# Two-matmul pairs between the blocks of a TensorE-bound transformer kernel, fewer split sums of squares, and two reordered pieces of scalar and vector work

## The chip, the cores and the metric

One core of a Trainium2 chip runs the whole program in one launch. The metric is the device time of an execution in microseconds, the median over several executions of the same kernel. Next to the timed executions stands one execution that was recorded by the hardware profiler.

## The reference

The input is one sequence of 256 tokens, 1024 wide, in fp32. A first half has two pre-norm layers: layer 0 mixes tokens by attention (eight stick-breaking heads, eight softmax heads), layer 1 by retention, and each is followed by a gated feed-forward network (FFN) of inner width 2816. A second half has two hybrid layers with a convolution branch, a latent-attention branch (MLA) and a dilated-attention branch of three groups, merged under gates. What the change touches is this, cut to its core:

```python
def rmsnorm(x, g):                       # sums of squares over the features
    return x * rsqrt(mean(x * x, -1) + eps) * g

def retention_mixer(h, w_in, gn_gain, w_o, pos):
    q, k, v, g = split(h @ w_in)         # q, k rotated; o normalised per head by mean of squares
    return (silu(g) * o) @ w_o

def swiglu(h, w_gate_up, w_down):
    gt, up = split(h @ w_gate_up)
    return (silu(gt) * up) @ w_down

def hybrid_layer(x, ...):
    proj = rmsnorm(x, norm_g) @ w_in
    dq, dk = rmsnorm(per head of 64)     # 24 tiles of 128 rows: dqk
    ...                                  # MLA scores, dilated scores, outputs
    merged = g_a * (y_a @ w_out_a) + g_b * (y_b @ w_out_b) + g_c * (y_c @ w_out_c)
    return x + merged @ w_o
```

## The kernel before

Everything lies transposed: features on the 128 partitions, the 256 tokens along the free axis. Each weight matrix is cut into blocks of 128x1024 values, eight 128x128 tiles in a block. A block is one DMA into `raw` (four slots). ScalarE copies it into a high part `whi` (L1158, `hi`), VectorE subtracts to get the low part `wlo` (L1670, `lo`), and TensorE multiplies each tile in three matmuls, high by high, high by low and low by high (L512, L513, L514 in `run`). A block is thus 24 matmuls with 256 moving columns of the rounded fp32 type. The moving operand is `h` (normalised x), `ah` (the gated product in the FFN), `yh` or `mh` (in the merges), each with its low half beside it. `run_late` does the same for the first two tiles of some output projections (L539 to L541). All engines follow an order written out by hand and meet at semaphores. A tile result lies in one of four slots in turn, `slot_free` tells that it was read, `blk_done` that a block's matmuls are over. The tile numbered g cannot begin before the tile g-2 was read, since two share a bank pair `G`.

Between the blocks stand short matmuls in plain fp32. They sum squares over partitions with a matrix of ones (`ones`, or `bones` with ones in each head's 64 rows). Plain fp32 matmuls have two records each in the trace. The places that matter here:

- `in_halves(to, w, moving, start)` issues a 256-column fp32 matmul as two of 128 columns (all on L898). It is called by `ret_sum` (retention norm), by `d_sums` (the 24 head norms of a hybrid layer, one after each block) and by `mla_scores`.
- `entry_sums` (L966, L967) sums squares at the entry of each hybrid layer, in halves.
- `ffn(b, g, n)` on TensorE runs `run_two`, two further blocks and then a hardware loop over 10 groups of four blocks; FFN1 has its first four blocks by themselves and then loops from the third group on. The `down` projection follows each FFN at once, without other work between.
- The merge of a hybrid layer is 4 x 3 turns of three blocks. Ahead of the second block of the first turn stands `pair_outs(7)`, the last attention output (L1102). In the first turn, ahead of the third block, TensorE waits on `y_lo` for the last low half of `yh`.
- The entry of the retention layer: blocks 0 to 3 run on x before it is normalised (`run_unnormed`), so their results are multiplied by 1/rms on VectorE (`by_root`, L1930) and get a shift added on ScalarE (L1372, a loop of four that waits for `q_scaled`). Only after that loop does ScalarE read out block 4 (L1401).
- The entry of FFN1 is alike. There VectorE has the products of group 0 (`up_gate` L2006, `up_low` L2012), then `ffn(..., first=1)`: for each half of a group `lo`, the product of gate and up (L1901), `lo`, the product's low half (L1905), and in some turns a reduction for the modulation vectors (L1678, by the table `FFN1_DOTS`).

## Time and profile before

| | us |
|---|---|
| timed executions | 1467.92, 1468.67, 1471.16 |
| median | 1468.67 |
| profiled execution, its own time | 1464.42 |
| its span, first to last instruction | 1462.6 |
| TensorE busy in the span | 1441.0 (99%) |
| VectorE busy | 1043.7 (71%) |
| ScalarE busy | 848.6 (58%) |
| mean granted TensorE clock | 0.997 |

The profiled execution's own time is 1.8 us more than its span. Its own time is also 4.25 us below the median of the timed ones and 3.5 us below the lowest. A matmul's duration in the trace is modelled and overlaps the next one's, so the pace of TensorE is to be read from starts, or from how many instructions a stretch holds, and not from busy time.

### The profile page before, as it was taken

Reading aid. Unit: us, or ns where it says so; the run is one execution under the profiler, and the core shown is the slowest. Engines: PE = TensorE matmul, PEld = TensorE weight load, DVE = VectorE, ACT = ScalarE, POOL = GpSimd, SP = SyncE. Lnnn points to the kernel's source line nnn. Section 1 sums busy time; section 2 is a strip of 40 time slices with the busy share of each in tenths; the row PEclk is TensorE's granted clock in tenths of the full one; section 3 lists DMA queues with packets and bytes.
Section 4 is the critical chain, followed back from the end, with each engine's and each line's share of the span. In section 5 each row is a group of like instructions: output and inputs, shape, how many; then the busy total and the mean of one; then the engine's idle time right before and its main releaser. Section 6 shows DMA issues by size and latency. Waiting matters only on the chain.

```text
span 1462.6 us, 30445 instructions
## 1 busy us (share of the span) xinstructions
PE 1441.0 (99%) x11704; PEld 1371.9 (94%) x11704; DVE 1043.7 (71%) x1861; ACT 848.6 (58%) x1482; POOL 92.0 (6%) x136
## 2 busy tenths in 40 slices
PE   8999999999999999999999999999999999999999
PEld 6887999999989999999998989899999898989999
DVE  2888898987776678765666757876576684787664
ACT  4465666555456756545566766554456675656543
POOL 0101011110000000000020000410000000031000
PEclk9999999999999999999999999999999999999999
DMA  9867699997665377666563554345666355434663
GB/s 364 325 208 224 218 337 336 340 348 229 200 233 156 116 216 228 190 191 196 188 232 117 162 169 145 97 123 185 190 189 209 115 172 165 143 96 130 188 200 118
DMA packets 81186, 292.06 MB, mean 200 GB/s; under 512 B 9185, under 2 KB 10465, under 8 KB 80946
## 3 DMA queue, kind: packets, MB, share of 16 engines
q1 hardware_dynamic: 68274, 244.31, 51.6%
q0 software_dynamic: 11792, 42.77, 8.8%
q10 hardware_dynamic: 1008, 3.41, 0.7%
q8 instruction: 80, 1.31, 0.4%
q14 instruction: 32, 0.26, 0.1%
HBM read 289.40 MB, written 1.05 MB: 199 GB/s over the span
## 4 chain that ended last, share of the span: by engine, by line
PE 89%; DVE 7%; ACT 2%; issue 2%; DMA 0%; SPq 0%; DVEq 0%; ACTq 0%
PE G L512 22%; PE G L513 22%; PE G L514 22%; PE G L571 3%; PE G L572 3%; PE G L573 3%; DVE wlo L1670 2%; PE Tp L898 2%; PE O L1102 1%; PE G L593 1%; ACT whi L1158 1%; PE Tp L952 1%; PE S L1004 1%; DVE aw L1678 1%; PE Tp L686 1%
## 5 line engine op out<-in xcount | busy, mean ns | idle before, releaser
L1670 DVE TENSOR_TENSOR wlo<-raw,whi 128x1024 fp32r<-128x1024 f32 x444 | 546.0, 1232 | 257.2 <-ACT whi L1158 255.4
L1158 ACT ACTIVATE whi<-raw 128x1024 fp32r<-128x1024 f32 x444 | 468.8, 1058 | 216.7 <-PE G L514 160.7
L512 PE MATMUL G<-h,whi 128*128 128x256 f32 x2064 | 583.5, 283 | 4.8 <-DVE at L2319 1.6
L513 PE MATMUL G<-h,whi 128*128 128x256 f32 x2064 | 572.8, 278 | 0.0
L514 PE MATMUL G<-h,wlo 128*128 128x256 f32 x2064 | 572.8, 278 | 0.0
L512 PEld LDWEIGHTS G<-h,whi 128*128 128x128 f32 x2064 | 389.4, 189 | 10.6 <-issue 2.2
L513 PEld LDWEIGHTS G<-h,whi 128*128 128x128 f32 x2064 | 388.0, 188 | 0.7 <-issue 0.5
L514 PEld LDWEIGHTS G<-h,wlo 128*128 128x128 f32 x2064 | 387.8, 188 | 0.0
L1678 DVE CUSTOM_DVE_ANT_0 aw<-aw,cs,cols 128x1024 f32<-128x1024 f32 x80 | 101.4, 1278 | 0.0
L512 PE MATMUL G<-ah,whi 128*128 128x256 f32 x352 | 97.2, 276 | 0.0
L513 PE MATMUL G<-ah,whi 128*128 128x256 f32 x352 | 97.2, 276 | 0.0
L514 PE MATMUL G<-ah,wlo 128*128 128x256 f32 x352 | 97.2, 276 | 0.0
L488 POOL TENSOR_TENSOR bias<-dist,slopes 128x256 f32<-128x256 f32 (+1 forms) x48 | 47.3, 1002 | 538.3 <-DVE mn L2272 528.8
L512 PE MATMUL G<-yh,whi 128*128 128x256 f32 x288 | 80.2, 278 | 0.0
L513 PE MATMUL G<-yh,whi 128*128 128x256 f32 x288 | 80.0, 278 | 0.0
L514 PE MATMUL G<-yh,wlo 128*128 128x256 f32 x288 | 80.0, 278 | 0.0
L571 PE MATMUL G<-whi,h 128*128 128x512 f32 x192 | 76.8, 400 | 1.4 <-ACT mqk L1267 1.4
L471 POOL DMA_DIRECT2D aw<-in_ada x80 | 42.4, 530 | 536.3 <-DVE mod L1678 502.0
L572 PE MATMUL G<-whi,h 128*128 128x512 f32 x192 | 75.6, 394 | 0.0
L573 PE MATMUL G<-wlo,h 128*128 128x512 f32 x192 | 75.6, 394 | 0.0
L512 PEld LDWEIGHTS G<-ah,whi 128*128 128x128 f32 x352 | 66.1, 188 | 0.0
L513 PEld LDWEIGHTS G<-ah,whi 128*128 128x128 f32 x352 | 66.1, 188 | 0.0
(408 smaller groups left out, 2334.1 us busy)
## 6 DMA issues: line engine op xcount, KB each, us to landing
raw<-in_w SPq DMA_DIRECT2D x444, 512.0 KB, 3.8
aw<-in_ada POOLq DMA_DIRECT2D x80, 512.0 KB, 5.4
adaw<-in_ada SPq DMA_DIRECT2D x8, 1024.0 KB, 15.5
sn<-in_uq ACTq DMA_DIRECT2D x2, 768.0 KB, 4.3
x<-in_x SPq DMA_DIRECT2D x1, 1024.0 KB, 5.3
pt<-in_ukv ACTq DMA_DIRECT2D x2, 512.0 KB, 5.4
out<-x SPq DMA_DIRECT2D x4, 256.0 KB, 2.3
dec<-in_dec ACTq DMA_DIRECT2D x1, 512.0 KB, 7.3
```

The lines of the kernel that those rows point to most:

```text
L471: pool.dma_start(aw[:, r % ADA_SLOTS, :], a["ada"][16 + r]).then_inc(ada_raw[r % ADA_SLOTS], 16)
L488: pool.tensor_tensor(bias[:, DIST[grp]], dist[:, DIST[grp]], slopes[:, c:c + 1].broadcast_to([P, w]), ALU.mult).then_inc(bias_ready, 1)
L512: pe.matmul(o, wh, mv[:, 0:T], start=(k == 0), stop=False)
L513: pe.matmul(o, wh, mv[:, T:2 * T], start=False, stop=False)
L514: ins = pe.matmul(o, wl, mv[:, 0:T], start=False, stop=(k == k_of - 1))
L571: pe.matmul(o, hh, wh, start=(k == 0), stop=False)
L572: pe.matmul(o, hl, wh, start=False, stop=False)
L573: ins = pe.matmul(o, hh, wl, start=False, stop=(k == KT - 1))
L898: ins = pe.matmul(to[:, o:o + P], w, moving[:, o:o + P], start=start, stop=True)
L1158: act.activation(whi[:, s, :], raw[:, s, :], ACT.Copy).then_inc(w_hi, 1)
L1670: dve.tensor_tensor(wlo[:, s, :], raw[:, s, :], whi[:, s, :], ALU.subtract).then_inc(w_lo, 1)
L1678: return dve.tensor_tensor_reduce(out=w, in0=w, in1=cs[:, :], scale=1.0, scalar=cols[:, C_ADAB + n:C_ADAB + n + 1], op0=ALU.mult, op1=ALU.add,
```

## The change

Five edits. (1) A new helper `settle` issues two 128-column fp32 matmuls of `ones` by `ones` into the bank `O`, whose content nobody reads. It is called four times: in `ffn` ahead of the loop (FFN0), ahead of FFN1's loop, and in each hybrid layer's merge ahead of the third block of the first turn. (2) Sums of squares stay in halves only where nothing but the sum stands between two blocks: `ret_sum` for head 3, `d_sums` for the tiles 3 and 5 to 17 (it is called with j-1). Elsewhere (three in retention, ten in each hybrid layer) they are one 256-column matmul. `entry_sums` has its first operand whole and its second in halves. (3) `mla_scores` issues the 256-column part first and whole, then the 128-column part. (4) ScalarE's four shifts at the retention entry move behind the read-out of blocks 5 and 6, two at each. (5) At FFN1's entry VectorE does the first gate product of group 1 right after the first low half of group 0, and the reductions start two halves later.

```diff
-FFN1_DOTS = {_f: [70 + _f] for _f in range(2, 10)}
+FFN1_DOTS = {_f: [68 + _f] for _f in range(4, 12)}
...
+            def settle():
+                for _ in range(2):
+                    pe.matmul(O[:, 0:P], ones[:, :], ones[:, :], start=True, stop=True)
...
                 run(b + 2, g + 2, 2, 8, of_h)
+                settle()
                 with pe.Fori(1, FT // 2) as i:
...
-                in_halves(Tp[:, slot, 0:T], ones[:, :], sq[:, 4, :], True).then_inc(t_done, 1)
+                if hh == 3:
+                    in_halves(Tp[:, slot, 0:T], ones[:, :], sq[:, 4, :], True).then_inc(t_done, 1)
+                else:
+                    pe.matmul(Tp[:, slot, 0:T], ones[:, :], sq[:, 4, :], start=True, stop=True).then_inc(t_done, 1)
...
             run(B_FFN1 + 4, G_FFN1 + 4, 4, 8, of_h, each_k=lambda k: pe.wait_ge(h_ready, 24 + k + 1))
+            settle()
             with pe.Fori(2, FT // 2) as i:
...
+                    pe.matmul(S[:, 2, 0:T], ones[:, :], sq[:, 0, :], start=True, stop=False)
                     for o in (0, P):
-                        pe.matmul(S[:, 2, o:o + P], ones[:, :], sq[:, 0, o:o + P], start=True, stop=False)
-                        ins = pe.matmul(S[:, 2, o:o + P], ones[:, :], sq[:, KT - 1, o:o + P], start=False, stop=True)
+                        ins = pe.matmul(S[:, 2, o:o + P], ones[:, :], sq[:, KT - 1, o:o + P], start=False, stop=(o == P))
...
-                        d_sums(j - 1)
+                        d_sums(j - 1, alone=j == 4 or 5 < j < 19)
...
-                    pe.matmul(S[:, slot, 0:P], q[:, 0:P], kk[:, 0:P], start=True, stop=True)
-                    in_halves(S[:, slot, P:384], q[:, P:T], kk, True).then_inc(s_done, 1)
+                    pe.matmul(S[:, slot, P:384], q[:, P:T], kk, start=True, stop=True)
+                    pe.matmul(S[:, slot, 0:P], q[:, 0:P], kk[:, 0:P], start=True, stop=True).then_inc(s_done, 1)
...
                             pe.wait_ge(y_lo, l * 12 + 12)
+                            settle()
...
-            for b in range(4):
+            def shift(b):
+
                 act.wait_ge(q_scaled, b + 1)
                 act.activation(rqk[:, b, :], rqk[:, b, :], ACT.Identity, bias=scol[:, b:b + 1]).then_inc(q_shifted, 1)
...
                 hi(B_RET + b + 4)
+                if b in (5, 6):
+                    shift(2 * b - 10)
+                    shift(2 * b - 9)
...
             up_low(0)
+            dve.wait_ge(ah_ready, FT + 1)
+            gate_product(B_FFN1, G_FFN1, 1, 0)
             up_low(1)
+            lo(B_FFN1 + 8)
+            lo(B_FFN1 + 9)
+            product_low(1, 0)
+            lo(B_FFN1 + 10)
             dve.wait_ge(ah_ready, FT + 2)
-            ffn(B_FFN1, G_FFN1, FFN1_DOTS, 1)
+            gate_product(B_FFN1, G_FFN1, 1, 1)
+            lo(B_FFN1 + 11)
+            product_low(1, 1)
+            ffn(B_FFN1, G_FFN1, FFN1_DOTS, 2)
```

On TensorE, in the first turn of hybrid layer 0's merge, at the border of the second block (moving operand `h`) and the third (`yh`), there stood:

```order
L514 MATMUL G<-h,wlo 128x256
L512 MATMUL G<-h,whi 128x256
L513 MATMUL G<-h,whi 128x256
L514 MATMUL G<-h,wlo 128x256
L512 MATMUL G<-yh,whi 128x256
L513 MATMUL G<-yh,whi 128x256
L514 MATMUL G<-yh,wlo 128x256
```

and there stands now, with the pair at the border:

```order
L514 MATMUL G<-h,wlo 128x256
L512 MATMUL G<-h,whi 128x256
L513 MATMUL G<-h,whi 128x256
L514 MATMUL G<-h,wlo 128x256
L857 MATMUL O<-ones 128x128 x2
L512 MATMUL G<-yh,whi 128x256
L513 MATMUL G<-yh,whi 128x256
L514 MATMUL G<-yh,wlo 128x256
```

The pair came between two blocks; nothing else moved there.

On ScalarE, at the retention entry (L1329 and L1344 are the read-out of a raw block, L1158 and L1173 `hi`, L1372 and L1388 the shifts, L1401 and L1417 the read-out of blocks 4, 5, 6, ...), before:

```order
L1329 ACTIVATE rqk<-G 128x256
L1158 ACTIVATE whi<-raw 128x1024 x2
L1372 ACTIVATE rqk<-rqk,hb 128x256 x4
L1401 ACTIVATE rqk<-G 128x256
L1158 ACTIVATE whi<-raw 128x1024
L1401 ACTIVATE rqk<-G 128x256
L1158 ACTIVATE whi<-raw 128x1024
L1401 ACTIVATE rqk<-G 128x256
```

and now:

```order
L1344 ACTIVATE rqk<-G 128x256
L1173 ACTIVATE whi<-raw 128x1024 x2
L1417 ACTIVATE rqk<-G 128x256
L1173 ACTIVATE whi<-raw 128x1024
L1417 ACTIVATE rqk<-G 128x256
L1173 ACTIVATE whi<-raw 128x1024
L1388 ACTIVATE rqk<-rqk,hb 128x256 x2
L1417 ACTIVATE rqk<-G 128x256
L1173 ACTIVATE whi<-raw 128x1024
L1388 ACTIVATE rqk<-rqk,hb 128x256 x2
L1417 ACTIVATE rqk<-G 128x256
```

The read-outs of blocks 4 and 5 passed all four shifts.

On VectorE, at FFN1's entry (L2006 and L2033 `up_gate`, L2012 and L2039 `up_low`, L1901 and L1918 the gate product, L1905 and L1924 its low half, L1670 and L1689 `lo`, `ISA` the reduction), before:

```order
L2006 SCALAR_TENSOR_TENSOR af<-af,hb,sg 128x256
L1670 TENSOR_TENSOR wlo<-raw,whi 128x1024
L2012 TENSOR_TENSOR ah<-af,ah 128x256 x2
L1670 TENSOR_TENSOR wlo<-raw,whi 128x1024
L1901 TENSOR_TENSOR af<-G,sg 128x256
L1670 TENSOR_TENSOR wlo<-raw,whi 128x1024
L1905 TENSOR_TENSOR ah<-af,ah 128x256
L1678 ISA aw,mod<-aw,cs,cols 128x1024
L1678 ISA mod 128x1
L1670 TENSOR_TENSOR wlo<-raw,whi 128x1024
```

and now:

```order
L2033 SCALAR_TENSOR_TENSOR af<-af,hb,sg 128x256
L1689 TENSOR_TENSOR wlo<-raw,whi 128x1024
L2039 TENSOR_TENSOR ah<-af,ah 128x256
L1918 TENSOR_TENSOR af<-G,sg 128x256
L2039 TENSOR_TENSOR ah<-af,ah 128x256
L1689 TENSOR_TENSOR wlo<-raw,whi 128x1024 x2
L1924 TENSOR_TENSOR ah<-af,ah 128x256
L1689 TENSOR_TENSOR wlo<-raw,whi 128x1024
L1918 TENSOR_TENSOR af<-G,sg 128x256
L1689 TENSOR_TENSOR wlo<-raw,whi 128x1024
L1924 TENSOR_TENSOR ah<-af,ah 128x256
L1689 TENSOR_TENSOR wlo<-raw,whi 128x1024
```

The first product passed an `up_low` and a `lo`, and two reductions left this stretch for later.

## Rows read from the trace of the kernel before

**Rows 1.** The page: its span, and its chain that ended last by engine

```profile
span 1462.6 us, 30445 instructions
...
PE 89%; DVE 7%; ACT 2%; issue 2%; DMA 0%; SPq 0%; DVEq 0%; ACTq 0%
```

**Rows 2.** Windows: length; busy (x count) PE, PEld, DVE, ACT, POOL; clock; DMA; GB/s

```profile
172.70:346.70 174.00, 174.00 (x1538) 174.00 (x1537) 154.35 (x219) 101.64 (x134) 23.22 (x44) 1.00 0.93 331
365.80:385.80 20.00, 20.00 (x171) 20.00 (x171) 14.86 (x13) 10.02 (x16) 0.00 (x0) 1.00 0.50 154
566.40:726.40 160.00, 160.00 (x1414) 160.00 (x1413) 106.70 (x140) 82.56 (x119) 1.58 (x3) 1.00 0.67 208
976.00:1072.00 96.00, 96.00 (x818) 96.00 (x817) 57.54 (x78) 47.05 (x65) 0.00 (x0) 1.00 0.58 182
...
1344.00:1440.00 96.00, 96.00 (x849) 96.00 (x848) 61.32 (x84) 49.37 (x67) 0.00 (x0) 1.00 0.64 189
1442.40:1459.00 16.60, 16.60 (x142) 16.60 (x142) 7.18 (x10) 3.49 (x4) 0.00 (x0) 1.00 0.16 61
```

**Rows 3.** Timeline of TensorE around two single sums in halves, hybrid layer 0

```profile
765.73 0.29 PE L513 MATMUL G<-h,whi 128*128 128x256 f32 x1
...
768.32 0.28 PE L514 MATMUL G<-h,wlo 128*128 128x256 f32 x1
768.45 0.61 PE L898 MATMUL Tp<-sq,bones 128*128 128x128 f32 x4
...
769.36 0.28 PE L513 MATMUL G<-h,whi 128*128 128x256 f32 x1
...
771.52 0.28 PE L514 MATMUL G<-h,wlo 128*128 128x256 f32 x1
...
786.58 0.28 PE L514 MATMUL G<-h,wlo 128*128 128x256 f32 x1
...
787.26 0.28 PE L513 MATMUL G<-h,whi 128*128 128x256 f32 x1
```

**Rows 4.** Timeline of TensorE: a 256-column fp32 matmul before a block

```profile
761.14 0.60 PE L985 MATMUL Tp<-csq,ones 128*128 128x256 f32 x2
...
761.69 0.28 PE L513 MATMUL G<-h,whi 128*128 128x256 f32 x1
```

**Rows 5.** Timeline at the retention entry, TensorE and then ScalarE

```profile
364.61 0.28 PE L514 MATMUL G<-h,wlo 128*128 128x256 f32 x1
365.58 0.38 PE L512 MATMUL G<-h,whi 128*128 128x256 f32 x1 [0.69 <-ACT rqk L1401]
365.80 0.28 PE L513 MATMUL G<-h,whi 128*128 128x256 f32 x1
...
359.79 2.01 ACT L1158 ACTIVATE whi<-raw 128x1024 fp32r<-128x1024 f32 x2
...
363.95 1.31 ACT L1372 ACTIVATE rqk<-rqk,hb 128x256 f32<-128x256 f32 x3 [0.96 <-DVE rqk L1930]
365.17 0.36 ACT L1401 ACTIVATE rqk<-G 128x256 f32<-128x256 f32 x1
```

**Rows 6.** Timeline at FFN1's entry, TensorE and then VectorE

```profile
564.63 0.28 PE L514 MATMUL G<-h,wlo 128*128 128x256 f32 x1
565.97 0.39 PE L512 MATMUL G<-h,whi 128*128 128x256 f32 x1 [1.06 <-DVE af L1901]
566.19 0.28 PE L513 MATMUL G<-h,whi 128*128 128x256 f32 x1
...
563.57 0.75 DVE L2012 TENSOR_TENSOR ah<-af,ah 128x256 fp32r<-128x256 f32 x2
564.35 1.23 DVE L1670 TENSOR_TENSOR wlo<-raw,whi 128x1024 fp32r<-128x1024 f32 x1
565.50 0.42 DVE L1901 TENSOR_TENSOR af<-G,sg 128x256 f32<-128x256 f32 x1
```

**Rows 7.** Timeline of VectorE: the last low half of `yh`, layer 0

```profile
974.91 0.43 DVE L2294 TENSOR_TENSOR yh<-hpair,yh 128x256 fp32r<-128x256 f32 x1 [0.15 <-ACT yh L1604]
```

More of the change, by code:

```diff
@@ L970, in entry_sums @@
                         pe.wait_ge(sqf_ready, 8)
+                        pe.matmul(S[:, 1, 0:T], ones[:, :], sqf[:, 0, :], start=True, stop=False)
                         for o in (0, P):
[L972 to L973 removed]
+                            ins = pe.matmul(S[:, 1, o:o + P], ones[:, :], sqf[:, KT - 1, o:o + P], start=False,
+                                            stop=(o == P))
                     ins.then_inc(ss_done, 1)
@@ L1020, in mla_transposes, with d_sums @@
                     ins.then_inc(t_done, 1)
-                def d_sums(j):
+                def d_sums(j, alone=False):
                     slot = use_t()
                     pe.wait_ge(d_sq, l * 24 + j + 1)
-                    in_halves(Tp[:, slot, 0:T], bones[:, :], sq[:, j % 8, :], True).then_inc(t_done, 1)
+                    if alone:
+                        in_halves(Tp[:, slot, 0:T], bones[:, :], sq[:, j % 8, :], True).then_inc(t_done, 1)
+                    else:
+                        pe.matmul(Tp[:, slot, 0:T], bones[:, :], sq[:, j % 8, :], start=True, stop=True).then_inc(t_done, 1)
                 pe.wait_ge(in_hyb, 64)
@@ L1892, in _, with gate_product, product_low @@
             x_update(B_ATT_O, 8, G_ATT_O, one_each, 2, 4, later={0: [21], 1: [22], 2: [23]})
+            def gate_product(b, g, i, q):
+                gg = g + 2 * q
+                dve.wait_ge(blk_done, b + 2 * q + 2 + 4 * i)
+                dve.wait_ge(slot_free[gg % 4], taken(gg) + i)
+                dve.tensor_tensor(af[:, q, :], gslot(gg + 1), sg[:, q, :],
+                                  ALU.mult).then_inc(slot_free[(gg + 1) % 4], 1)
+            def product_low(i, q):
+                dve.wait_ge(ah_hi, ah_base[0] + i * 2 + q + 1)
+                dve.tensor_tensor(ah[:, i * 2 + q, T:2 * T], af[:, q, :], ah[:, i * 2 + q, 0:T],
+                                  ALU.subtract).then_inc(ah_ready, 1)
             def ffn(b, g, later, first=0):
```

12 lines of the change are left out of this document (2 added, 10 removed).

## The prediction

> **What bounds the kernel now.** I read the page first: its chain is TensorE for 89% and VectorE for 7% [rows 1]. So a saved matmul interval is saved time, and work on the other engines counts only where TensorE is seen to wait for it. Next I read TensorE's stream in windows, since its durations are modelled, and divided each window's length by its count of matmuls. A count includes those under way at the window's start, so I add one duration, 0.28 us, to the length [rows 2, 5]. FFN0 with its down projection: 174.28/1538 = 113.3 ns from start to start. FFN1: 160.28/1414 = 113.4. The merge of hybrid layer 1: 96.28/849 = 113.4. The merge of layer 0, the same code on the same shapes: 96.28/818 = 117.7 [rows 2]. Twenty microseconds at the retention entry (20.28/171 = 118.6, its uneven first intervals included) and the last 16.6 us of the program (16.88/142 = 118.9, its edges included) are of the slow kind too. The granted clock is 1.00 in all of them, its 2.4 GHz level, and TensorE is busy for the whole window, so neither the clock nor a wait explains it: the same stream has two paces, 4.35 ns a matmul apart, and it keeps the one that it has for hundreds of matmuls.
>
> What sets the pace? At two single sums in halves: before the first one 22 intervals take 768.32 - 765.73 = 2.59 us, 117.7 ns each, and after it 19 take 771.52 - 769.36 = 2.16, 113.7 by rounded starts [rows 3]. One pair of 128-column fp32 matmuls alone between blocks took the stream from slow to fast. There are 28 such places in the two hybrid layers. A stall works differently: after the one at the retention entry the pace is slow [rows 2, 5], after the one at FFN1's entry fast [rows 2, 6]. I read the pace after a stall as chance, which is an inference from those two.
>
> **The settling pairs (+1.8, -3.7 us).** What one costs: from the last matmul before the sum to the second after it 787.26 - 786.58 = 0.68 us, where two intervals without it would be 0.23, so 0.45 [rows 3]. Four of them are 1.8 us on the path. Nothing waits for bank `O` there, and `settle` adds no wait. In layer 0's merge the pair stands behind the wait on `y_lo`; that half was ready at 974.91 + 0.43 = 975.34, and the block in front of the pair begins at 973.9 and lasts 2.8 us, so this wait stays covered [rows 7]. What they bring: in layer 0's merge 34 blocks of 24 matmuls follow, 816 x 4.35 ns = 3.55 us, and some 48 matmuls of the output projection, 0.2 us, if the slow pace lasted until there: 3.7 us. ScalarE and VectorE can feed the fast pace, since they do so in layer 1 [rows 2]; were they late, the loss would be up to those 3.7. In layer 1's merge, FFN0 and FFN1 the profiled execution is fast already, so there the pair only costs. At the end of a merge the pace changes once more: in layer 1 the last 142 matmuls are slow behind a fast merge [rows 2]. If layer 0's output projection now does the same, 142 x 4.35 = 0.6 us come back; I count half, +0.3, bounds 0 and 0.6.
>
> [...]
>
> **The shifts (-1.7 us).** TensorE's block 6 begins late: from its predecessor's start to its own second matmul it is 365.80 - 364.61 = 1.19 us instead of 0.23, a stall of 0.96. It waited for ScalarE's read-out of block 4, which began at 365.17, behind the shifts, which wait for VectorE's `by_root` [rows 5]. Block 5 began 24 intervals (2.72) ahead of 364.73, at 362.0, so block 4 was over by about 362.1, and ScalarE was free of its two `hi` at 359.79 + 2.01 = 361.80. Without the shifts it reads block 4 out at 362.2 to 362.6, two microseconds before block 6 wants the slot. The next to be late could be `lo` of block 8, wanted at 364.7 + 2 x 2.72 = 370.2. Its `hi` (1.0 us) now ends near 363.6, its `lo` (1.2 us) follows VectorE's `by_root`, at about 366. Blocks 5 and 6 carry two shifts each afterwards, 2 x 0.4 us in a block of 2.7, beside one `hi` and one read-out: 2.2 us, which fits. So all 0.96 goes. With the stall goes what it left behind, since I saw the pace before it to be fast: some 171 slow matmuls x 4.35 = 0.74. Bounds 0.96 (the slow pace comes otherwise) and 1.7; I take 1.7, as nothing else interrupts the stream there.
>
> **The gate product (-1.35 us).** TensorE's block 7 stalls alike: 566.19 - 564.63 = 1.56 instead of 0.23, so 1.33, for the product at L1901. VectorE was busy up to it: the two low halves (563.57, 0.75 us), then `lo` (564.35, 1.23 us), then the product at 565.50 [rows 6]. Now the product stands behind the first low half, at about 563.95, and ends near 564.35, before block 7 wants the slot at 564.74. That is a margin of 0.4 us. Should the extra wait for the own low half cost 0.1, it still holds; should the product come 0.5 us late, 0.1 of the stall stays. Behind it `lo` of block 8 ends near 566.0 (wanted 567.5), of block 9 near 567.1 (wanted 570.2), the second product follows block 7 and `lo` of block 10, near 568.9, for a slot wanted at 570.2. Two reductions (1.28 each) moved out of this stretch make that room and are taken up later in a loop that has it. I take 1.33, bounds 1.2 and 1.35.
>
> **Whole sums and the score order (-0.5 us).** One 256-column fp32 matmul before a block: 761.69 - 761.14 = 0.55 us to the block's second matmul [rows 4]. The pair takes from its own start, one interval (0.12) behind 786.58, 787.26 - 786.70 = 0.56 [rows 3]. So each of 23 sums saves 0.01 to 0.02 us, as do 16 score pairs and 3 groups at the entries: 42 x 0.015 = 0.6, from 0.4 to 0.8. What pace the next block has is the larger unknown. Behind these places stand some 40 blocks of 24 matmuls, 0.10 us each between the two paces, part slow today and part fast: from -2 to +2 us if all went one way. The single pairs were kept where they work, and a pair with other work behind it shows nothing that it loses, so I take 0 for this and -0.5 for the edit.
>
> **The sum.** +1.8 - 3.7 + 0.3 - 1.7 - 1.35 - 0.5 = -5.15. The profiled execution's own time would go from 1464.42 to 1459.3.
>
> The timed executions lie 3.5 to 6.7 us above the profiled one, and the pace explains that without any other cause: in the profile FFN0, FFN1 and layer 1's merge were all fast. Slow, they would cost 1538 x 4.35 = 6.7 us, 1414 x 4.35 = 6.2 and 849 x 4.35 = 3.7 [rows 2]. The median is 4.25 above, about one merge; the highest is 6.7 above, one FFN. If that is so, the pairs pin all four stretches, and the timed executions of the changed kernel come down to its profiled one, with some 0.7 us for the short stretches that stay free: **1460.0 us**. If the 4.25 is a fixed difference of a recorded execution, the time is 1468.67 - 5.15 = 1463.5.
>
> **The rivals.** *Fixed difference*: 1463.5, as just worked out. For it speaks that all three timed executions lie above the recorded one; against it that two stretches of like code differ by just that amount. *The pair does not hold the pace*: it sets the next block fast, and the stream falls back, or the pace is set by something later. Then the 3.7 stay and the pairs cost 1.8: 1468.67 + 1.8 + 0.3 - 1.7 - 1.35 - 0.5 = 1467.2, about no change. [...] Against it speaks that fast stretches last 170 us [rows 2]; for it that none of the 28 pairs has more than one block behind it before the next short matmul. *Slower*: the state that a pair leaves depends on what it is issued from, and behind a branch into a hardware loop it is the slow one. FFN0 and FFN1, now fast, would lose 6.7 + 6.2 = 12.9 us, fixed in each execution: 1463.5 + 12.9 = 1476.4. It decides from about 8 us, so it takes both FFNs, or one with layer 0's merge unmended. No pair in the trace stands at such a branch.
>
> **How the numbers follow.** A measurement of this kernel can tell about 0.2%, 2.9 us. Pinned paces, 1457 to 1462: 55%. Fixed difference, 1462 to 1465.5: 28%. The pair does not hold: 12%, of which most within 2.9 us of before. Slower: 4%; 1% is for what I don't see. The range 1457 to 1465.5 holds the first two, 83%. Faster by over 0.2%: the first two and a little of the third, 86%; the same 10%; slower 4%.
>
> **What would show it.** In the changed profile the windows of layer 0's merge, layer 1's merge, FFN0 and FFN1 must all give 113.4 ns a matmul. The stalls before blocks 6 and 7 of the two entries must be gone, with 113 ns through the retention entry. The pair must cost 0.45. The timed executions must lie closer to the profiled one and to each other than 3.5 and 3.2 us. I am wrong if a stretch behind a pair runs at 117.7, if VectorE's new order shows a wait for `lo` of block 8 or 9, or if the 40 short blocks turned slow.

## The result and the profile after

The changed kernel takes 1478.38 us, median of 8 runs (1473.26 to 1481.88); the kernel before, beside it on the same chip, 1466.84 us (1463.35 to 1471.91, 8 runs). The ratio is 1.0079, 95% interval 1.0051 to 1.0106: slower, where 1460.0 and a range of 1457 to 1465.5 were predicted. The profiled execution took 1481.88 us. The ratios, here and below, compare whole sets of executions; where a set is skewed they differ from the quotient of the two medians, by up to 0.003. One execution of e12_ones_at_64 below took 2048.87 us at a granted clock of 0.65 and is left out of that run's numbers. The page of after, its span and its chain that ended last (compare [rows 1]):

```profile
span 1480.1 us, 30308 instructions
...
PE 87%; DVE 8%; ACT 3%; issue 2%; DMA 1%; SPq 0%; DVEq 0%; ACTq 0%
```

TensorE still bounds. Windows of after (length; busy time and count of PE, PEld, DVE, ACT, POOL; clock, DMA share, GB/s): FFN0 with its down projection, the retention entry, FFN1, the two merges, the last 16.6 us (compare [rows 2]):

```profile
180.00:350.00 170.00, 170.00 (x1445) 170.00 (x1445) 145.75 (x208) 94.62 (x125) 22.47 (x43) 1.00 0.93 323
368.00:388.00 20.00, 20.00 (x179) 20.00 (x178) 14.82 (x17) 12.04 (x20) 0.00 (x0) 1.00 0.67 209
577.00:735.00 158.00, 158.00 (x1344) 158.00 (x1343) 100.61 (x131) 77.57 (x112) 1.58 (x3) 1.00 0.64 200
992.00:1088.00 96.00, 96.00 (x817) 96.00 (x817) 58.63 (x81) 46.44 (x63) 0.00 (x0) 1.00 0.61 187
1360.00:1456.00 96.00, 96.00 (x817) 96.00 (x816) 58.65 (x81) 46.68 (x64) 0.00 (x0) 1.00 0.60 186
1459.90:1476.50 16.60, 16.60 (x143) 16.60 (x143) 7.18 (x10) 3.45 (x4) 0.00 (x0) 1.00 0.16 60
```

With 0.28 us added to each length, as in the prediction: 170.28/1445 = 117.8 ns a matmul in FFN0, 158.28/1344 = 117.8 in FFN1, 96.28/817 = 117.8 in both merges. All four stretches behind a settling pair are slow. The retention entry, which has no pair, is fast: 20.28/179 = 113.3. The granted clock is 1.00 in all of them, and TensorE has no idle time in any, so once more neither clock nor wait tells the paces apart.

The timeline of TensorE around FFN0's pair in after: two rows some distance ahead, the rows at the pair, two rows behind:

```profile
172.99 0.28 PE L512 MATMUL G<-h,whi 128*128 128x256 f32 x1
...
175.48 0.28 PE L513 MATMUL G<-h,whi 128*128 128x256 f32 x1
...
178.31 0.28 PE L514 MATMUL G<-h,wlo 128*128 128x256 f32 x1
178.43 0.60 PE L857 MATMUL O<-ones 128*128 128x128 f32 x4
178.79 0.36 PE L512 MATMUL G<-h,whi 128*128 128x256 f32 x1
178.99 0.28 PE L513 MATMUL G<-h,whi 128*128 128x256 f32 x1
...
181.11 0.28 PE L513 MATMUL G<-h,whi 128*128 128x256 f32 x1
...
183.70 0.28 PE L514 MATMUL G<-h,wlo 128*128 128x256 f32 x1
```

Between the first two rows lie 22 intervals: 2.49/22 = 113.2 ns. Between the last two lie 22 as well: 2.59/22 = 117.7. The pair itself costs what was predicted, 178.99 - 178.31 = 0.68 us where 0.23 stood. What it leaves is the opposite: it took a fast stream and made it slow. The other three do the same (FFN1's at 575.17, the merges' at 989.96 and 1357.46: fast in front, slow behind), and the pace then stays for 1390, 863 and 863 matmuls.

I counted every start-to-start interval between two 256-column matmuls of the stream: 116 to 122 ns is slow, up to 114 ns fast. Before has 2339 slow intervals, which is 10.4 us above the fast pace; after has 6276, which is 28.0 us. The difference is 17.5 us, and so is that of the spans, 1480.1 - 1462.6. The four stretches behind the pairs alone are 1486 + 1390 + 863 + 863 = 4602 slow intervals, 20.5 us. In before the one of layer 0's merge was slow already, so 3739 of them, 16.7 us, are new.

The two stalls that the other edits were made for are gone. ScalarE in after at the retention entry, and VectorE and TensorE at FFN1's (compare [rows 5, 6]):

```profile
369.52 0.38 ACT L1417 ACTIVATE rqk<-G 128x256 f32<-128x256 f32 x1 [0.40 <-PE G L514]
372.24 0.38 ACT L1417 ACTIVATE rqk<-G 128x256 f32<-128x256 f32 x1 [1.38 <-PE G L514]
...
373.47 0.90 ACT L1388 ACTIVATE rqk<-rqk,hb 128x256 f32<-128x256 f32 x2
```

```profile
571.73 0.42 DVE L1918 TENSOR_TENSOR af<-G,sg 128x256 f32<-128x256 f32 x1
572.07 0.41 DVE L2039 TENSOR_TENSOR ah<-af,ah 128x256 fp32r<-128x256 f32 x1
```

```profile
572.34 0.28 PE L514 MATMUL G<-h,wlo 128*128 128x256 f32 x1
572.45 0.28 PE L512 MATMUL G<-h,whi 128*128 128x256 f32 x1
572.56 0.28 PE L513 MATMUL G<-h,whi 128*128 128x256 f32 x1
```

ScalarE now waits for TensorE at each read-out and not the other way round, with the shifts in the gap behind. The product ends at 572.15, 0.3 us before TensorE's block 7 begins at 572.45, and its matmuls follow at 0.11.

### The profile page after: what moved, and what is told of

It is laid out like the page before. It is cut to its first block, busy times and chain, and to the rows that moved or that the text cites. A ratio compares the mean times of both kernels' runs of the same rounds, so it can differ in the third digit from the quotient of the medians.

```text
span 1480.1 us, 30308 instructions
## 1 busy us (share of the span) xinstructions
PE 1459.9 (99%) x11636; PEld 1387.2 (94%) x11636; DVE 1043.9 (71%) x1861; ACT 847.6 (57%) x1482; POOL 92.6 (6%) x136
## 4 chain that ended last, share of the span: by engine, by line
PE 87%; DVE 8%; ACT 3%; issue 2%; DMA 1%; SPq 0%; DVEq 0%; ACTq 0%
PE G L512 22%; PE G L514 21%; PE G L513 21%; DVE wlo L1689 2%; PE G L571 2%; PE G L573 2%; PE G L572 2%; ACT whi L1173 1%; PE O L1116 1%; PE Tp L904 1%; PE G L593 1%; PE Tp L962 1%; DVE aw L1697 1%; PE S L1015 1%; PE Tp L686 1%
## 5 line engine op out<-in xcount | busy, mean ns | idle before, releaser
L1689 DVE TENSOR_TENSOR wlo<-raw,whi 128x1024 fp32r<-128x1024 f32 x444 | 545.9, 1232 | 265.9 <-ACT whi L1173 264.2
L1173 ACT ACTIVATE whi<-raw 128x1024 fp32r<-128x1024 f32 x444 | 468.3, 1057 | 229.5 <-PE G L514 172.8
L513 PE MATMUL G<-ah,whi 128*128 128x256 f32 x352 | 98.9, 281 | 0.0
L512 PE MATMUL G<-ah,whi 128*128 128x256 f32 x352 | 98.9, 281 | 0.0
L513 PEld LDWEIGHTS G<-ah,whi 128*128 128x128 f32 x352 | 67.6, 192 | 0.0
L514 PEld LDWEIGHTS G<-ah,wlo 128*128 128x128 f32 x352 | 66.1, 188 | 0.0
```

The lines of the kernel that those rows point to most:

```text
L512: pe.matmul(o, wh, mv[:, 0:T], start=(k == 0), stop=False)
L513: pe.matmul(o, wh, mv[:, T:2 * T], start=False, stop=False)
L514: ins = pe.matmul(o, wl, mv[:, 0:T], start=False, stop=(k == k_of - 1))
L1173: act.activation(whi[:, s, :], raw[:, s, :], ACT.Copy).then_inc(w_hi, 1)
L1689: dve.tensor_tensor(wlo[:, s, :], raw[:, s, :], whi[:, s, :], ALU.subtract).then_inc(w_lo, 1)
```

## The experiments

A pair of the head norms (stationary matrix `bones`) had been seen to leave a fast stream; the settling pair (stationary matrix `ones`) left a slow one. In what do they differ? The head norms' pair is two halves of one sum with operand `sq`, it stands behind waits, it signals a semaphore, it writes bank `Tp`, and its stationary matrix is another tensor. In what follows F is the fast pace (113.3 ns), S the slow one (117.8), and F to S means that the stream was fast in front of an insertion and slow behind it, read in the block on either side. All medians have the kernel before measured beside them, on the same chip.

**e1_no_pairs, e2_pairs_alone, e3_pairs_as_sums, s1_kinds.** The first takes all `settle()` calls out of the changed kernel; the second puts only the four pairs into the kernel before; the third writes the pair like a head norm's sum; the fourth puts 68 pairs of seven kinds between the blocks of both merges of the kernel before.

```diff
 # e1 (the changed kernel; at all four places)
-                        settle()
 # e2 (the kernel before), s1: settle() at the four places, pair(kind) at 68
+                            settle()
 # e3 (the changed kernel)
-                for _ in range(2):
-                    pe.matmul(O[:, 0:P], ones[:, :], ones[:, :], ...)
+                pe.wait_ge(in_ones, 16)
+                for o in (0, P):
+                    ins = pe.matmul(O[:, o:o + P], ones[:, :], sq[:, 0, o:o + P], ...)
+                ins.then_inc(settled, 1)
```

> The changed kernel without its four settling pairs. Theory A (the pair of ones by ones leaves the slow pace behind it, and the four long stretches pay for it): the two stalls stay gone, nothing forces the four stretches, each has either pace by chance; the time is about 0.8 to 1.2% below the changed kernel's, 1460 to 1467 us, and the profile has 117.8 ns in at most two or three of the four. Rival B (the slow pace comes from the other edits, the whole sums, the score order or the missing stalls): the four stretches stay at 117.8 and the time stays near 1477.

> The kernel before with the four pairs and nothing else. Theory A: all four stretches run at 117.8 ns behind the pair, and with 1.8 us for the pairs and the stalls kept the time is 1478 to 1484 us, above the changed kernel's. Rival B: the pace is as before, 1467 to 1470.

> The changed kernel with each pair written as the head norms' pair is: squares as moving operand, two halves of the bank, a wait that is met already ahead of it, an increment behind it. Theory A1 (what the pair consists of decides): 113.4 ns in all four stretches and 1457 to 1463 us. Rival A2 (the place decides, such as the 24-matmul blocks around it and what the next waits are, not the pair's form): 117.8 ns in all four as in the changed kernel, 1476 to 1480.

> A screening on the kernel before: in both merges a pair between every two blocks from the third on, 68 in all, of seven kinds in two orders: plain as in the change; two halves of the bank; a met wait ahead; an increment behind; squares as moving operand; halves, wait and increment; all four. The next block's pace is read from each. If one property decides, its kinds give 113 ns and the others 118 whatever the pace was before; if the place decides, kinds do not differ. The time is about 68 x 0.45 = 31 us above before and more with slow blocks.

Without the pairs: 1464.45 us (1458.57 to 1475.62, 12 runs) beside 1467.23, ratio 0.9993 [0.9965, 1.0022]. So the pairs are the loss. In e1's profile all four stretches are fast. The pairs alone: 1475.3 us (1473.16 to 1487.05), ratio 1.0087 [1.0058, 1.0116], the whole loss of the change. Its profile shows what the changed kernel's could not: the pair does not make the stream slow, it turns the pace. FFN0 went F to S, FFN1 S to F, the first merge S to F, the second F to S. Windows of e2 in these four stretches:

```profile
180.00:347.00 167.00, 167.00 (x1420) 167.00 (x1419) 142.75 (x204) 93.32 (x123) 22.27 (x42) 1.00 0.92 323
577.00:735.00 158.00, 157.65 (x1391) 157.45 (x1390) 103.85 (x137) 80.84 (x117) 1.06 (x2) 1.00 0.66 206
986.00:1082.00 96.00, 96.00 (x850) 96.00 (x849) 60.35 (x83) 48.63 (x66) 0.00 (x0) 1.00 0.63 192
1350.00:1446.00 96.00, 96.00 (x818) 96.00 (x817) 57.90 (x79) 46.18 (x64) 0.00 (x0) 1.00 0.61 186
```

167.28/1420 = 117.8 and 96.28/818 = 117.7 behind the two that were fast; 96.28/850 = 113.3 in the first merge. Written as a sum, the pair turns the pace as well: e3 took 1476.95 us (1475.99 to 1481.57), 1.0086 [1.0059, 1.0114], with F to S, S to F, F to S, F to S. In s1, one execution of 1497.31 us, 68 of 68 insertions turned it, whatever the kind (plain, halves, met wait, increment, `sq` operand, and their sums), with 677 ns from the last matmul in front to the second behind for F to S and 685 for S to F. The form of the sum is out. All of these stand in an unbroken stream. One pair with `ones` in every kernel stands behind a stall, the last sum of retention, with 0.96 to 1.28 us over the insertion, and there all four outcomes occur: F to F in after and e1, F to S in e4 and e6, S to F in before and e2, S to S in e3 and e9.

**s2_kinds, e4_two_waits, e5_two_pairs, e6_orders_alone.** s2 is a second set of 68 insertions: one to four matmuls, two met waits ahead, the head norms' bank, `bones` as stationary matrix. e4 and e5 are the changed kernel with two met waits ahead of each pair, and with four matmuls at each place. e6 is the kernel before with the moved shifts and the moved product alone.

```diff
 # s2 (the kernel before), in both merges at each border of blocks
+                            pair(next(kinds))
 # e4
+                pe.wait_ge(in_ones, 16)
+                pe.wait_ge(in_c, 32)
                 for _ in range(2):
 # e5
-                for _ in range(2):
+                for _ in range(4):
 # e6 (the kernel before), ScalarE; VectorE's half is that of the change
+                if b in (5, 6):
+                    shift(2 * b - 10)
+                    shift(2 * b - 9)
```

> So far a pair of 128-column fp32 matmuls has always turned the pace round (72 of 72 outside the head norms), whatever its operands, bank, single wait or increment, while the head norms' pairs give the fast pace from either. Screening on the kernel before, 34 insertions in each merge in random order: 2 matmuls; 2 behind two met waits; 1, 3, 4 matmuls; one of 256 columns, without and with two waits; 2 with the head norms' matrix; 2 in the head norms' bank. Theory W (the two waits ahead of a head norm's pair make the difference): only the kinds with two waits give the fast pace from either state, the matrix and the bank turn round. Rival M (the matrix or the bank does): those kinds give fast from either. For the number: if each 128-column matmul shifts a phase, 1 and 3 keep or turn as 2 does not, and 4 keeps the pace.

> The changed kernel with two met waits ahead of each pair. Theory W: the two FFN stretches run at 113.4 ns in each execution (the merges have a third wait there already and may differ), and the time is 1456 to 1464 us. Rival M: the pair turns the pace as before, 1475 to 1480 us.

> The changed kernel with two pairs in a row at each of the four places. If a pair turns the pace round, two keep it: the stretches run at what they had ahead of the pairs, mostly fast, and the time is 1462 to 1470 us with 3.6 us for the pairs. Rival (fp32 work of any length leaves the slow pace): 117.8 ns in all four, 1478 to 1482.

> The kernel before with the moved shifts and the moved gate product alone. Theory: both stalls of 0.96 and 1.33 us are gone in the profile, and the stretches behind them have the pace that the stream had ahead of them; the median is 2 to 4 us under before, with a spread of some 10 us between executions that can hide it. Rival: the stalls come back elsewhere, the time is as before.

What s2 showed (one execution, 1499.55 us), by kind. The entries give the pace behind the insertion, first where the stream in front was fast, then where it was slow:

```
                                     from F         from S
one 128-column matmul, ones          F 4 of 4       F 1, S 1
three, ones                          F 4 of 4       F 1, S 1
two, ones, two met waits ahead       S 8 of 8       F 5 of 5
two, ones, in the head norms' bank   S 6 of 6       F 2 of 2
two, ones                            S 5 of 5       F 3 of 3
two, bones                           F 2 of 2       F 6 of 6
four, ones                           -              F 6 of 6
one 256-column, ones                 S 8 of 8       F 4, S 1
```

Two 128-column matmuls with `ones` turned the pace every time, four did so from a slow stream, one or three left a fast stream fast and had both answers from a slow one. A 256-column fp32 matmul turned the pace in 12 of 13 cases. Waits and bank count for nothing, but with `bones` a pair leaves the stream fast. e4 took 1474.81 us, 1.005 [1.0024, 1.0075]: the theory of the waits falls. e5 took 1475.53 us, 1.0036 [1.0007, 1.0064], with F to S three times and S to F once: four matmuls turn the pace as two do, and that two pairs would keep it was a miss. e6 took 1466.8 us, 1.0001 [0.997, 1.0031], its runs spread over 20 us (1457.99 to 1478.52): its retention entry is fast and free of the stall, and its FFN1 happened to be slow for 1438 matmuls, 6.4 us, more than the edits bring. With the pace left free, small edits can't be measured in this kernel.

**s3_matrices, e7_single.** s3 varies the stationary matrix alone in 68 insertions; e7 is the changed kernel with one matmul at each place instead of two.

```diff
 # s3 (the kernel before), w: ones, bones, ident or dist[:, c:c + P]
+                for k in range(n):
+                    pe.matmul(O[:, 0:P], w, ones[:, :], start=True, stop=True)
 # e7
-                for _ in range(2):
+                for _ in range(1):
                     pe.matmul(O[:, 0:P], ones[:, :], ones[:, :], start=True, stop=True)
```

> The screening so far: two met waits change nothing (13 of 13 turned the pace round), the bank neither (8 of 8), but with the head norms' matrix as stationary operand the pair gave the fast pace 8 times of 8, twice from the fast one. Here the stationary operand varies, 68 insertions on the kernel before: ones, head norms' matrix, identity, and 128-column pieces of the distance table that begin 0, 16, 32, 64 and 3584 bytes into it; also a single matmul with either of the first two. Theory P (place in the memory: ones, identity and the piece at 64 bytes begin on a multiple of 128 bytes, the head norms' matrix and the pieces at 0 and 3584 half way between two): the latter three give fast from either pace, the former three turn it round. Rival C (content, mostly zeros): the head norms' matrix and the identity give fast, all pieces of the table turn it round.

> The changed kernel with one 128-column matmul of ones by ones in place of each pair. In the screening one matmul kept the fast pace (4 of 4) and gave the fast one in one of two cases from the slow pace. So the two FFN stretches and the merge stretches, fast ahead of it, stay at 113.4 ns where the pair turned them: 1457 to 1466 us. Rival: at these places one matmul does what two do, 1475 to 1480 us.

In s3 (one execution, 1493.7 us) a pair with the identity turned a fast stream in 5 of 5 cases, like `ones`, and so did a piece of the distance table (6 of 6); other pieces of the same table, 32 to 64 bytes earlier, left it fast (9 of 9), as `bones` did (3 of 3). So it isn't what the matrix holds, it is where it lies. `ones`, the identity and the piece that turns start 128 bytes into a stretch of 256 in their partition's memory, as do the weight tiles `whi` and `wlo`; `bones` starts at 64. A single matmul with `ones` left a fast stream fast (4 of 4) and, here, a slow one slow (2 of 2); a single one with `bones` made it slow (5 of 5), the reverse of what the two do as pairs.

e7 took 1459.44 us (1458.31 to 1461.66, 12 runs) beside 1467.46 (1460.98 to 1472.75), **ratio 0.9954 [0.994, 0.9969]: faster than both kernels**, by 0.5% against before, with a spread of 3.4 us where before has 11.8. The timeline of e7 at FFN1's single matmul:

```profile
567.66 0.28 PE L514 MATMUL G<-h,wlo 128*128 128x256 f32 x1
567.77 0.38 PE L857 MATMUL O<-ones 128*128 128x128 f32 x2
567.91 0.37 PE L512 MATMUL G<-h,whi 128*128 128x256 f32 x1
568.11 0.28 PE L513 MATMUL G<-h,whi 128*128 128x256 f32 x1
```

and windows of e7: FFN0, the retention entry, FFN1, the merges:

```profile
180.00:347.00 167.00, 167.00 (x1476) 167.00 (x1475) 147.74 (x211) 97.52 (x129) 22.79 (x43) 1.00 0.94 335
361.00:384.00 23.00, 23.00 (x205) 23.00 (x204) 17.76 (x21) 14.22 (x23) 0.00 (x0) 1.00 0.59 184
569.00:725.00 156.00, 156.00 (x1379) 156.00 (x1378) 103.83 (x137) 80.69 (x117) 1.59 (x3) 1.00 0.66 208
977.00:1073.00 96.00, 96.00 (x849) 96.00 (x848) 60.47 (x84) 48.34 (x66) 0.00 (x0) 1.00 0.63 194
1341.00:1437.00 96.00, 96.00 (x849) 96.00 (x849) 60.34 (x83) 48.27 (x65) 0.00 (x0) 1.00 0.63 193
```

The single costs 568.11 - 567.66 = 0.45 us where 0.23 stood, and 167.28/1476, 23.28/205, 156.28/1379 and 96.28/849 are 113.3, 113.6, 113.3 and 113.4 ns: all these stretches are fast. Three of the singles went F to F, and FFN0's, in front of which the stream was slow, S to F. With those of s2 and s3 that makes 2 of 5 slow streams that a single with `ones` mended, so why all twelve executions lie so close together is not shown. This is the state that the prediction had forecast for the pair, at the time that it had forecast.

**e8_ones_moved, e9_singles_alone, e10_bones_aligned.** e8 moves the ones matrix 64 bytes further in the changed kernel (and all tensors behind it by 128); e9 is the kernel before with the four single matmuls only; e10 is the kernel before with `bones` moved from 64 to 128 bytes into 256 (and all tensors behind it by 128).

```diff
 # e9 (the kernel before, settle() at the four places)
+                for _ in range(1):
+                    pe.matmul(O[:, 0:P], ones[:, :], ones[:, :], start=True, stop=True)
 # e8
+        sb("pad_a", [P, 16])
         ones = sb("ones", [P, P])
+        sb("pad_b", [P, 16])
 # e10
+        sb("pad_c", [P, 16], stack=second)
         bones = sb("bones", [P, P], stack=second)
+        sb("pad_d", [P, 16], stack=second)
```

> The changed kernel with the matrix of ones 64 bytes further in the memory, nothing else. Theory P (a pair whose stationary matrix does not begin on a multiple of 128 bytes leaves the fast pace): 113.4 ns behind all four settling pairs, and 1457 to 1462 us with a spread of some 4 us. Rival (the pair's place in the program counts too, or the content): the four stretches stay slow, 1475 to 1480 us.

> The kernel before with one 128-column matmul of ones by ones at each of the four places. Both FFN stretches and the merges keep the fast pace where they come in fast. Against e7_single it still has the two stalls (0.96 and 1.33 us, and a pace by chance behind each until the single) and the split sums (0.5 us): 1461 to 1464 us. Rival: the other edits are worth nothing, 1459 to 1460.

> The kernel before with the head norms' matrix on a multiple of 128 bytes (64 further). Theory P: its single pairs between blocks now turn the pace round, so the blocks of the head norms alternate between 113.4 and 117.8 ns where they were all fast, some 14 slow blocks more, 1.5 us. Rival C (content): they all stay fast.

e8 took 1484.68 us (1481.66 to 1485.68), 1.0114 [1.0084, 1.0145]: a miss. Its pairs went F to S three times and S to F once, and the head norms' 28 pairs, whose `bones` had moved to 192 as well, left the stream slow in 28 of 28 cases, in each of which it had come in slow. A pair at 192 bytes does not leave the stream fast, so the rule on record for e8 (every place but the multiples of 128 bytes leaves it fast) is wrong. e10 met its expectation: in the kernel before these 28 pairs leave the stream fast, every one; with `bones` at 128 they turn it, every one, 16 times F to S and 12 times S to F. Two of them in a row, timeline of TensorE in e10:

```profile
792.16 0.28 PE L516 MATMUL G<-h,wlo 128*128 128x256 f32 x1
792.27 0.60 PE L900 MATMUL Tp<-sq,bones 128*128 128x128 f32 x4
792.63 0.36 PE L514 MATMUL G<-h,whi 128*128 128x256 f32 x1
792.83 0.28 PE L515 MATMUL G<-h,whi 128*128 128x256 f32 x1
...
795.42 0.28 PE L516 MATMUL G<-h,wlo 128*128 128x256 f32 x1
795.54 0.61 PE L900 MATMUL Tp<-sq,bones 128*128 128x128 f32 x4
795.91 0.37 PE L514 MATMUL G<-h,whi 128*128 128x256 f32 x1
796.11 0.28 PE L515 MATMUL G<-h,whi 128*128 128x256 f32 x1
...
798.62 0.28 PE L516 MATMUL G<-h,wlo 128*128 128x256 f32 x1
```

From a block's second matmul to its last lie 22 intervals: (795.42 - 792.83)/22 = 117.7, then (798.62 - 796.11)/22 = 114.1 with the uneven first ones. The profiled execution of e10 has a span of 1473.6, its one time is 1475.45 us. e9 took 1464.65 us, 0.9987 [0.9969, 1.0005], with a spread of 5.5 us: F to F at all four singles, and still the stall and the slow pace at the retention entry.

**s4_places, e11_mask_pair, e12_ones_at_64.** s4 takes ten places within one matrix, the distance table. e11 gives the pair of the changed kernel another stationary matrix, the causal mask, at 32 bytes into 256, and moves nothing. e12 moves the ones matrix to 64, and keeps all tensors behind it at their places into 256.

```diff
 # s4 (the kernel before): w = dist[:, c:c + P], ten values of c
 # e12
+        sb("pad_a", [P, 48])
         ones = sb("ones", [P, P])
+        sb("pad_b", [P, 16])
 # e11
-                    pe.matmul(O[:, 0:P], ones[:, :], ones[:, :], start=True, stop=True)
+                    pe.matmul(O[:, 0:P], cmask[:, 0:P], ones[:, :], start=True, stop=True)
```

> The kernel before with 68 pairs between blocks in the merges, each pair with a stationary matrix that starts at one of ten places, given as bytes into 256: 64, 96, 112, 128, 144, 160, 192, 224, 0 and 32; all are pieces of one matrix, and nothing else differs between the kinds. The stream's weight tiles lie at 128. Theory of the place (relative to the weight tiles, in pieces of 256 bytes): the piece at 128 turns the pace every time, those at 64, 96 and probably 32 and 112 leave it fast from either pace, those at 192 and probably 160 and 224 leave it slow from either. Rival, that the place counts only through a multiple of 128 bytes: 128 and 0 turn the pace, and all other places leave it fast. Rival, that place does not count and the outcomes so far were chance: every kind shows all outcomes.

> The changed kernel with the causal mask's first 128 columns as the pairs' stationary matrix, at 32 bytes into 256 where the ones lie at 128; nothing is moved. If the place decides: the stream is fast behind all four pairs, so 20.5 us come back less what the four places of the kernel with single matmuls also had, and the time is 1458 to 1462 us, ratio about 0.995 to 0.997, with a spread of some 4 us. If the pair itself turns the pace whatever its matrix: as the changed kernel, 1470 to 1482 us.

> The changed kernel with the ones matrix 192 bytes further, at 64 into 256, and all tensors behind it 256 bytes further, so that these keep their own places into 256. If the place decides: fast behind all four pairs as with the mask, 1458 to 1464 us, and the head norms' pairs still leave the stream fast. The head sums and rms sums in two halves also use the ones matrix and would now leave it fast too. If the effect of moving the ones in the earlier run came from the tensors behind it: the four pairs turn the pace, or leave it slow, and the time is 1470 us or more.

Pairs of s3 and s4 (one execution, 1498.92 us) together, by the place of their stationary matrix (bytes into 256):

```
place   from F          from S             ns over the insertion, from F (s4)
  0     S  5 of  5      S 2 of 2           676-677
 32     F  4 of  4      F 1, S 1           682
 64     F  9 of  9      F 15, S 2          683-684
 80     F  4 of  4      F 2 of 2
 96     F 11 of 11      F 4 of 4           681-682
112     S  3 of  3      F 3 of 3           679
128     S 24 of 24      F 6 of 6           676-677
144     F  2 of  2      F 5 of 5           682
160     F  6 of  6      F 2 of 2           688-689
192     S  3 of  3      F 2, S 2           679
224     S  2 of  2      F 2, S 2           686
```

From a fast stream each place gave its own answer every time, in 73 of 73 insertions. The places 64 and 128 stand for three different addresses each, the other nine for one each, some with only two or three insertions. From a slow one four places gave both answers, so something else counts there too. None of the three theories on record fits: not halves of 256 bytes, not multiples of 128, not chance. The insertion as a whole takes 676 to 689 ns by the place, and the pace behind goes with that time, though not in order (676 to 679 and 686 give S, 681 to 684 and 688 to 689 give F).

e11 took 1460.81 us (1458.22 to 1462.21, 12 runs) beside 1464.43 (1460.68 to 1476.87, 23 runs), ratio 0.9957 [0.9936, 0.9979]. The same two matmuls at the same four places, with another matrix read, bring the time from 1.0079 to 0.9957 of before. Behind all four the stream is fast, at FFN1's after a slow one (S to F), at the others after a fast one. Windows of e11 in FFN0, FFN1 and a merge:

```profile
180.00:347.00 167.00, 167.00 (x1476) 167.00 (x1476) 147.64 (x212) 97.54 (x129) 22.71 (x43) 1.00 0.95 334
...
569.00:725.00 156.00, 156.00 (x1379) 156.00 (x1378) 103.43 (x137) 80.58 (x117) 1.58 (x3) 1.00 0.67 207
977.00:1073.00 96.00, 96.00 (x849) 96.00 (x849) 60.36 (x83) 48.53 (x66) 0.00 (x0) 1.00 0.64 193
```

e12 took 1465.08 us (1459.67 to 1473.51, 9 runs), 0.9999 [0.9971, 1.0028], between both of its expectations. In its profile both merges' pairs went F to F and both FFNs' S to S; windows of e12, FFN0 (170.28/1445 = 117.8 ns) and the first merge (90.28/797 = 113.3):

```profile
180.00:350.00 170.00, 170.00 (x1445) 170.00 (x1445) 145.78 (x208) 94.67 (x125) 22.56 (x43) 1.00 0.92 324
992.00:1082.00 90.00, 90.00 (x797) 90.00 (x796) 56.22 (x78) 45.51 (x62) 0.00 (x0) 1.00 0.64 193
```

A pair at 64 keeps a fast stream fast and does not always mend a slow one, as in the table.

**All profiled executions but the four screenings.** Take from each span what its slow intervals cost above the fast pace:

```
                    span     slow intervals   their excess   span less excess
e7_single           1457.4   1416              6.3           1451.1
e11_mask_pair       1457.9   1035              4.6           1453.3
e1_no_pairs         1458.3   1662              7.4           1450.9
before              1462.6   2339             10.4           1452.2
e9_singles_alone    1463.4   2042              9.1           1454.3
e6_orders_alone     1464.6   3079             13.8           1450.8
e2_pairs_alone      1471.4   3906             17.4           1454.0
e12_ones_at_64      1471.7   4472             19.9           1451.8
e10_bones_aligned   1473.6   4495             20.0           1453.6
e3_pairs_as_sums    1474.2   4779             21.2           1453.0
e5_two_pairs        1474.2   4529             20.1           1454.1
e4_two_waits        1477.5   5390             24.0           1453.5
after               1480.1   6276             28.0           1452.1
e8_ones_moved       1483.0   7153             31.9           1451.1
```

The spans differ by 25.6 us, the last column by 3.5. Most of what tells these kernels apart is the pace.

## Why the prediction was wrong

**The step that failed.** "One pair of 128-column fp32 matmuls alone between blocks took the stream from slow to fast." As a reading of `bones` pairs it holds: all 28 in the kernel before leave a fast stream. (Only 4 of them came from a slow one, 24 came in fast and stayed fast.) The error was to carry it to a pair with another stationary matrix, as if "two short fp32 matmuls" were all that there is to it. With `ones` a pair turns the pace (s1, 68 of 68; e2), because of where that matrix lies (s3, s4, e10, e11). The term "-3.7" for what the pairs bring came out as +16.7 us against the profile of before, or +20.5 against a stream that had stayed as it was in front of each pair. Layer 0's merge, which was to give the 3.7, stayed slow. Layer 1's merge, FFN0 and FFN1, of which the prediction said that each "is fast already, so there the pair only costs", became slow: 863, 1486 and 1390 matmuls, which had been put at nothing.

**The paces.** That the stream has two, 113.4 and 117.7, that it keeps one for hundreds of matmuls, and that the granted clock and waits don't tell them apart: right, and larger than supposed, since 22 of the 25.6 us between fourteen profiled kernels are this.

**What a pair costs**, 0.45: right (0.68 - 0.23 in after).

**The shifts and the gate product.** Both stalls are gone, and the retention entry is fast, as worked out; the margin of the product was 0.3 us, where 0.4 was forecast. Their worth shows only where the pace is pinned: with single matmuls at the four places, the kernel with all other edits (e7) has the ratio 0.9954 and the one without (e9) 0.9987, a difference of 0.0033 or 4.8 us, where the shifts, the product and the sums were put at 1.7 + 1.35 + 0.5 = 3.55. These two ratios come from different sessions and are known to about 0.0015 and 0.0018 either way, so 3.55 is not excluded.

**Whole sums.** Their own price was right: in s2 an insertion of one 256-column matmul takes 661 to 662 ns from a fast stream and one of two 128-column ones 676 to 677, so a whole sum saves 0.015 us. Their pace term was taken as 0 within -2 to +2. Without the pairs the whole rest of the change gave 0.9993 [0.9965, 1.0022], which doesn't tell. A 256-column fp32 matmul with `ones` turned a fast stream in 8 of 8 cases, so such sums do choose the pace of the block behind; I didn't measure them by themselves.

**Layer 0's output projection**, put at +0.3 with bounds 0 and 0.6: fast in before, it is slow in after, for 142 matmuls, so the upper bound came true. Layer 1's is slow in both (16.88/143 = 118.0 in after).

**The spread.** "If that is so, the pairs pin all four stretches, and the timed executions of the changed kernel come down to its profiled one": wrong of these pairs, which turn the pace and so pass on whatever came in, and right of insertions that leave a fast stream fast. e7's executions lie within 3.4 us and its profiled one among them; before and e6, where nothing pins, spread over 11.8 and 20.5 us. So the rival of a fixed difference falls; two of the further executions of before, 1463.35 and 1463.6, lie below the profiled one, 1464.42. The rival of a pair that doesn't hold falls too: the pace held for up to 1486 matmuls.

**The rival that came true in part.** "The state that a pair leaves depends on what it is issued from" gave 1476.4, near to what came, with 4%. The nearness is partly luck, as it had both merges fast and both are slow. And the branch into a hardware loop isn't the cause: the merges' pairs, which stand at none, turned as well, and the insertions of e7 and e11 stand at the same branches and leave a fast stream. Its reason for being unlikely, that the trace shows no such pair, should have been applied to the matrix: the trace of before has one pair with `ones` alone between blocks, the last sum of retention at 499.61, and that one came from a slow stream and stood behind a short stall (0.97 us over the insertion instead of 0.68). None came from a fast one.

**What the Trainium skill says.** Its page "TensorE: Matmul & The Clock Gate", section "Back-to-back issue gap", gives N/2.4 + 2.5 ns, 109 ns for 256 columns, for matmuls by themselves. In a stream with a weight load ahead of each, it says, the two together set the spacing, about 81 ns at 128 columns and 131 ns at 512. For such a stream it has no figure at 256 columns, and no second pace for one shape. Here 113.3 and 117.8 ns were measured for this shape at one granted clock, in every kernel.

**What stays open.** Why the place of the short matmuls' matrix counts, by what rule over 256 bytes (the table has no simple period), why a slow stream has more than one answer, what sets the pace behind a stall, and whether the places of the weight tiles and of the moving operands matter as much; the weight tiles were not moved, and the moving operands not by themselves.

## What to carry to other kernels

Before one reads a difference of under 1% in a TensorE-bound kernel, the start-to-start intervals of the main stream should be counted by pace: here they explained 22 of 25.6 us between the profiled kernels, and without them edits worth some 3 us couldn't be seen. A trick seen to work in one place should be copied with all of its operands, the stationary matrix and its address too, or be read as a new experiment. The one to use here is a single 128-column fp32 matmul with `ones`, at 128 bytes into 256, at each entry of a long stretch, for 0.22 us each. Together with the other edits it gave 0.9954 of the time before and a spread of 3.4 us instead of 11.8; by itself it gave 0.9987 [0.9969, 1.0005], which is no sure gain, and a spread of 5.5 us. With `bones`, at 64, a single one made a fast stream slow (5 of 5).

## What the runs showed of the hardware

- A stream of 256-column matmuls with a weight load each runs at 113.3 or at 117.8 ns from start to start, at granted clock 1.00, and keeps its pace for up to 1540 intervals (before's FFN0, fast; 1486 slow intervals in the FFN0 of after) with no idle time between.
- Short fp32 matmuls between two blocks bear on the pace behind them: with `ones`, one or three keep a fast stream fast (12 of 12, s2 and s3), two in an unbroken stream turn it from either pace (29 of 29 in s2, 68 of 68 in s1). From a slow stream one matmul has both answers (F 2, S 3 in s2, s3 and e7).
- The place of the short matmuls' stationary matrix in memory, in steps as small as 16 bytes, decides what a pair does to a fast stream (73 of 73), and also the insertion's own time, 676 to 689 ns. Moving `bones` by 64 bytes changed what all 28 of its pairs do (e10).
